# Token attention in the order plain, differential, neighbourhood mixer; one square root for both differential groups

## The reference

```
oa, oa_t = mixer_a(...)    # plain: 8 query heads, softmax over 768 keys
ob, ob_t = mixer_b(...)    # neighbourhood: 4 heads, a window of the 512 tokens by a bias, and the context
oc, oc_t = mixer_c(...)    # differential: 4 heads, w = p[0] - lam * p[1], then rms_norm(o, g_sub)
x = x + gt1_x * (concatenate([oa, ob, oc]) @ w_out[l])
```

## Time and profile before

| | |
|---|---|
| median of three executions | 3666.6 us (3666.44 to 3673.21) |
| profiled execution: its time | 3661.56 us |
| its span (first to last instruction) | 3659.7 us |
| TensorE busy | 3528.0 us, 96% of the span |
| VectorE, ScalarE, GpSimd busy | 48%, 42%, 40% |
| token attention, layer 0 | from 240.8 us to 474.7 us |
| token attention, layer 1 | from 1334.2 us to 1563.2 us |

### The profile page before, as it was taken

The page is one execution under the profiler, slowest core; times in us unless marked ns, Lnnn a source line. Parts: engine busy times, 40 slices in busy tenths (PEclk is TensorE's granted clock), DMA queues, the critical chain, the costliest instruction groups (busy, mean ns, idle before and its releaser), DMA issues.

```text
span 3659.7 us, 50085 instructions
## 1 busy us (share of the span) xinstructions
PE 3528.0 (96%) x19796; PEld 2799.3 (76%) x19796; DVE 1755.0 (48%) x2922; ACT 1524.8 (42%) x2557; POOL 1458.4 (40%) x986
## 2 busy tenths in 40 slices
PE   7999889999999999899999989999999989999998
PEld 5776567888899766578887768878887768888886
DVE  5766645423334766633542776161114686162114
ACT  4445554433455446534332355443223355443222
POOL 4520014444588510034444435344444444434442
PEclk8999999999999999999999999999999999999999
DMA  7613513333365411423333213223333213323331
GB/s 230 161 48 115 174 35 93 93 98 96 105 185 173 114 45 42 155 87 101 93 98 96 76 34 104 81 73 95 97 94 81 75 41 87 98 61 101 93 98 58
DMA packets 642466, 355.59 MB, mean 97 GB/s; under 512 B 70469, under 2 KB 614841, under 8 KB 642233
## 3 DMA queue, kind: packets, MB, share of 16 engines
q1 hardware_dynamic: 630379, 339.66, 32.2%
q10 hardware_dynamic: 11854, 12.72, 1.1%
HBM read 346.28 MB, written 6.05 MB: 96 GB/s over the span
## 4 chain that ended last, share of the span: by engine, by line
PE 89%; DVE 5%; ACT 3%; issue 2%; DMA 1%; POOL 1%; SPq 0%; ACTq 0%; DVEq 0%
PE psum L876 67%; PE psum L1105 5%; PE psum L1136 3%; PE psum L1156 2%; PE psum L900 1%; DVE neg_max L2013 1%; PE psum L1077 1%; ACT work L1574 1%; PE psum L980 1%; PE psum L904 1%; PE psum L1185 1%; PE psum L1036 1%; PE psum L931 1%; PE psum L1163 1%; PE psum L1015 1%
## 5 line engine op out<-in xcount | busy, mean ns | idle before, releaser
L859 POOL TENSOR_TENSOR w_lo<-w_raw,w_hi 128x256 fp32r<-128x256 f32 (+3 forms) x936 | 1396.5, 1512 | 2126.3 <-ACT w_hi L1413 2126.0
L876 PE MATMUL psum<-h_hi,w_hi 128*128 128x512 f32 (+1 forms) x2736 | 1034.2, 378 | 2.5 <-POOL w_lo L859 1.5
L876 PE MATMUL psum<-h_lo,w_hi 128*128 128x512 f32 (+1 forms) x2736 | 1010.1, 369 | 0.0
L876 PE MATMUL psum<-h_hi,w_lo 128*128 128x512 f32 (+1 forms) x2736 | 1010.1, 369 | 0.0
L1413 ACT ACTIVATE w_hi<-w_raw 128x1024 fp32r<-128x1024 f32 (+1 forms) x546 | 570.9, 1047 | 622.5 <-PE psum L876 587.6
L876 PEld LDWEIGHTS psum<-h_hi,w_hi 128*128 128x128 f32 x2736 | 516.5, 189 | 112.0 <-issue 19.8
L876 PEld LDWEIGHTS psum<-h_lo,w_hi 128*128 128x128 f32 x2736 | 516.5, 189 | 94.7 <-issue 9.9
L876 PEld LDWEIGHTS psum<-h_hi,w_lo 128*128 128x128 f32 x2736 | 516.2, 189 | 87.4
L876 PE MATMUL psum<-hid_hi,w_hi 128*128 128x512 f32 (+1 forms) x1040 | 393.0, 378 | 1.8 <-POOL w_lo L859 1.7
L876 PE MATMUL psum<-hid_lo,w_hi 128*128 128x512 f32 (+1 forms) x1040 | 391.8, 377 | 0.0
L876 PE MATMUL psum<-hid_hi,w_lo 128*128 128x512 f32 (+1 forms) x1040 | 391.8, 377 | 0.0
(11 more groups left out here) (248 smaller groups left out, 4280.1 us busy)
## 6 DMA issues: line engine op xcount, KB each, us to landing
w_raw<-in_w_up_dram SPq DMA_DIRECT2D x132, 512.0 KB, 3.8
w_raw<-in_w_ff_dram SPq DMA_DIRECT2D x128, 512.0 KB, 3.8
w_raw<-in_w_in_dram SPq DMA_DIRECT2D x92, 512.0 KB, 3.9
w_raw<-in_w_ada_dram SPq DMA_DIRECT2D x80, 512.0 KB, 4.2
w_raw<-in_w_down_dram SPq DMA_DIRECT2D x48, 512.0 KB, 3.6
w_raw<-in_w_mkv_dram SPq DMA_DIRECT2D x32, 512.0 KB, 3.9
w_raw<-in_w_down_dram SPq DMA_DIRECT2D x24, 384.0 KB, 3.1
w_ada_first<-in_w_ada_dram SPq DMA_DIRECT2D x4, 2048.0 KB, 18.0
```

What stands on the lines that cost most here:

```text
L859: m = nc.gpsimd.tensor_tensor(WL[:, c % NSPLIT, k:k + step, :], RAW[:, c % NRAW, k:k + step, :], WH[:, c % NSPLIT, k:k + step, :].bitcast( ...
L876: m = pe.matmul(out_ap, lhs(a, k), rhs(b, k), start=(k == 0 and n == 0), stop=(k == nk - 1 and n == 2))
```

## The change

The token plan is now 0 to 15 plain, 16 to 31 differential (groups 4 and 5), 32 to 39 neighbourhood (groups 6 and 7). The context plan keeps its order. The modulation ends with i = 31 and so starts four steps earlier: i = 8 to 31 in layer 0, 16 to 31 in layer 1. One square root over both groups' statistics (16 columns) stands at i = 35, and one reciprocal; the spreads stand at i = 36 and 37.

```
-ADA_LAST = 36
+ADA_LAST = 32
...
+            if stream == "x":
+                differential()
+                window()
+            else:
+                window()
+                differential()
...
+        def std_at(att):
+
+            return max(i for i, o in att["ends"].items() if att["groups"][o]["diff"] is not None) + 4 if att["wide"] else None
+
         def spread_at(att, i):
 
-            diff = [o for o, g in enumerate(att["groups"]) if g["diff"] is not None]
-            return [o for n, o in enumerate(diff) if i == len(att["steps"]) + 2 * n]
+            if att["wide"]:
+                return [o for n, o in enumerate(diff_groups(att)) if i == std_at(att) + 1 + n]
+            return [o for n, o in enumerate(diff_groups(att)) if i == len(att["steps"]) + 2 * n]
...
-                        pe.wait_ge(*at("sub_rstd", (S, o)))
+                        pe.wait_ge(*at("sub_rstd", S if att["wide"] else (S, o)))
...
+                    if att["wide"] and i == std_at(att):
+                        act.wait_ge(*at("sub_taken", (S, groups[diff_groups(att)[-1]]["bank"])))
+                        nc.scalar.activation(SUBS[:, :, :], SUBS[:, :, :], ACT.Sqrt, bias=EPSC[:, 0:1],
+                                             scale=1.0 / HEAD).then_inc(*mark("sub_std", S))
...
-                        if o and g["diff"] is None:
-                            dve.wait_ge(*at("o_lo", (S, o - 1)))
+                        if g["diff"] is None and plain_before(att, o) is not None:
+                            dve.wait_ge(*at("o_lo", (S, plain_before(att, o))))
...
+                    if att["wide"] and i == std_at(att):
+                        dve.wait_ge(*at("sub_std", S))
+                        nc.vector.reciprocal(SUBS[:, :, :], SUBS[:, :, :]).then_inc(*mark("sub_rstd", S))
```

More of the change, by code:

```diff
@@ L613, in attention_plan_1 @@
                 groups.append(dict(tile=m, diff=None))
[L614 to L632, removed]
+            def window():
+                for j in range(2):
+                    for t in range(nt):
+                        adds = [[], []]
+                        if stream == "x":
+                            adds = [[(0, SEQ, TB[:, 2 * j + lane, 6 - 2 * t:14 - 2 * t, :].rearrange("p a b -> p (a b)"))]
+                                    for lane in range(2)]
+                        steps.append(dict(lanes=[rows(64 * lane, 64, 5 + j, 7 + j, t) for lane in range(2)], nk=nk, adds=adds,
+                                          mix=None))
+                        turns.append(dict(parts=[(len(steps) - 1, 0), (len(steps) - 1, 1)], v=values(P + 128 * j), t=t,
+                                          group=len(groups)))
+                    groups.append(dict(tile=4 + j, diff=None))
@@ new lines, in differential @@
+            def differential():
+                for j in range(2):
+                    for t in range(nt):
+                        for e in range(2):
+                            steps.append(dict(lanes=[rows(64 * e + 32 * m, 32, 9 + j, 11 + j, t) for m in range(2)], nk=nk,
+                                              adds=[[], []], mix=layer))
+                        turns.append(dict(parts=[(len(steps) - 2, 1), (len(steps) - 1, 1)], v=values(384 + 128 * j), t=t,
+                                          group=len(groups)))
+                    groups.append(dict(tile=6 + j, diff=layer))
@@ L755, in finish_plan, with diff_groups, plain_before @@
             return att
+        def diff_groups(att):
+            return [o for o, g in enumerate(att["groups"]) if g["diff"] is not None]
+        def std_at(att):
+            return max(i for i, o in att["ends"].items() if att["groups"][o]["diff"] is not None) + 4 if att["wide"] else None
         def spread_at(att, i):
-            diff = [o for o, g in enumerate(att["groups"]) if g["diff"] is not None]
-            return [o for n, o in enumerate(diff) if i == len(att["steps"]) + 2 * n]
+            if att["wide"]:
+                return [o for n, o in enumerate(diff_groups(att)) if i == std_at(att) + 1 + n]
+            return [o for n, o in enumerate(diff_groups(att)) if i == len(att["steps"]) + 2 * n]
+        def plain_before(att, o):
+            before = [n for n in range(o) if att["groups"][n]["diff"] is None]
+            return before[-1] if before else None
         def sub_stats(att, o):
@@ L2071, in attend @@
                         lo("o_lo", (S, o), att_out(att, o, HL), diff_out(att, o), att_out(att, o, HH))
+                    if att["wide"] and i == std_at(att):
+                        dve.wait_ge(*at("sub_std", S))
+                        nc.vector.reciprocal(SUBS[:, :, :], SUBS[:, :, :]).then_inc(*mark("sub_rstd", S))
                     for o in spread_at(att, i):
-                        dve.wait_ge(*at("sub_std", (S, o)))
-                        nc.vector.reciprocal(sub_stats(att, o), sub_stats(att, o)).then_inc(*mark("sub_rstd", (S, o)))
+                        if not att["wide"]:
+                            dve.wait_ge(*at("sub_std", (S, o)))
+                            nc.vector.reciprocal(sub_stats(att, o), sub_stats(att, o)).then_inc(*mark("sub_rstd", (S, o)))
                         dve.wait_ge(*at("sub_spread", (S, o)))
```

2 lines of the change are left out of this document (1 added, 1 removed).

## The result

The changed kernel takes 3676.3 us (median of 20 runs, 3670.6 to 3689.7), the one before 3666.6 (20 runs beside it). The ratio is 1.0022, with a 95% interval of 1.0015 to 1.0029: **8.1 us slower, 5.5 to 10.6**. The forecast was 3667, a change too small to be told from none, with a range of 3658 to 3677. One of e10's 12 executions took 6983.69 us and is left out of its ratio.

What follows compares the result with a forecast made beforehand. TensorE was taken as the bound, carrying 89% of the chain. Layer 0's steps +9.0, layer 1's +3.0, ends -11.8, next stage -1.8 and slower clock +2 summed to +0.4 us: median 3667, range 3658 to 3677.

Steps and rivals of the forecast that it cites:

- The ends: From the last exponentials to TensorE's next stage: 5.6 us in each layer, -11.8 us in all.
- The start of the next stage: Projection of layer 1, behind a fuller end: -1.8 us there, nothing in layer 0.
- The plain steps: Steps 8 to 16: 53.6 us in layer 0 with more modulation, +4.3; 43.4 in layer 1, down from 44.72.
- The differential steps: Differential steps in their new place: +0.4 us in layer 0 for modulation in the last four, -0.6 in layer 1.
- Steps 32 to 39: Neighbourhood steps, now last: 55.3 us in each layer, added up step by step from queue waits.
- ScalarE's queue in step 36: Two table loads, square root, two copies and split delay step 36's exponentials: step 36 takes 6.9 us, +0.9.
- the table rival: Each of two table switches in both layers costs a second price of 1.28 us: +5, 3672 us; chance 8%.
- matmuls at half speed in these steps: Sign that the forecast is wrong: matmuls of the last steps running at TensorE's lower clock level.
- the wait in i = 34: TensorE's middle transpose waits for VectorE's copy of the sums of squares; extra price 1 us a layer, +2.
- The wait in i = 34 decides: Rival: that 2 us gap drops TensorE to 1.2 GHz, some 4.5 us a layer: +7 to +9, median 3674.5; chance 17%.
- Inner costs hidden: Rival: neighbourhood steps' idle time hides queued work and waits overlap: -8 us, 3658 and a tick; chance 17%.
- The modulation doesn't fit: Rival: modulation in the last four differential steps costs 3.9 us a layer, not 0.4: +7, 3673.5; chance 8%.

Runs made afterwards that it cites:

- e10: Changed kernel plus two filler matmuls over constants in each of TensorE's gaps at i = 32 and i = 34: 1.0007 against the kernel before, +2.6 us.
- e9: e8 with the modulation ending with step 33 instead of 31: 0.9980 against the kernel before, -7.3 us.
- e1: Kernel before with one edit, the modulation ending with step 31 instead of 35: 1.0019 against the kernel before, +7.0 us.
- e5: Changed kernel unchanged, run and profiled a second time: 1.0021 against the kernel before, +7.7 us.
- e11: Kernel before unchanged, profiled a second time: 3670.47 us.
- e6: Changed kernel with ScalarE's split of the first two w_out chunks in steps 33 and 34 instead of 36 and 37: 1.0021 against before, +7.7 us.
- e8: Changed kernel with the edits of e3, e6 and e7 together: 0.9996 against the kernel before, -1.5 us.
- e3: Changed kernel with VectorE's copy of the sums of squares between the step's two lanes instead of behind both: 0.9998 against before, -0.7 us.
- e7: Changed kernel with the spreads at i = 37 and 38 instead of 36 and 37: 1.0013 against the kernel before, +4.8 us.
- e4: Changed kernel with the square root at i = 40 and the spreads at 41 and 42, behind all steps: 1.0018 against before, +6.6 us.

## Why the prediction was right or wrong

**The ends: right.** 5.47 and 5.55 us where 5.6 was said. The chain of after goes through the steps that were named, in layer 1:

```profile
1569.09 0.66 PE psum L1159 x4
1569.75 1.46 PE psum L1179 x24
1571.21 0.59 PE psum L1159 x4
1571.79 1.02 PE psum L1208 x16
1572.82 1.31 PE psum L1179 x24
1574.13 43.74 PE psum L899 x192
```

**The start of the next stage: right.** The projection takes 43.74 us instead of 45.55, which is the -1.8 to the hundredth; windows over both ends have a clock of 1.00, where it was 0.85.

**The plain steps: right.** 53.7 us (mean of two) for steps 8 to 16 where 53.6 was said; 43.35 in layer 1 where 43.4 was.

**The differential steps: half right.** 83.7 forecast in layer 0, 85.7 measured; 82.7 and 82.1 in layer 1. The 2 us too much in layer 0 are in steps 26 and 27, behind the wait for the squares of the first differential group; the window of 387.40 above shows the clock of 0.54.

**Steps 32 to 39: right at full clock, wrong as they ran.** With the gaps filled (e10) they take 55.12 us in each layer; 55.3 was forecast. Step by step, forecast and e10 (layer 0): step 33 7.5 and 7.61; 35 7.7 and 7.28; 36 6.9 and 6.72; 37 7.4 and 7.56; 38 7.8 and 7.63; 39 6.1 and 5.96. ScalarE's queue in step 36, which the forecast wrote down row by row, stands in the timeline of after so:

```profile
448.96 1.28 ACT L1603 ACT_TABLE_LOAD   x1
450.26 0.31 ACT L1603 ACTIVATE sub_stats<-sub_stats,eps_cols 128x16 f32<-128x16 f32 x1
450.47 0.58 ACT L1567 ACTIVATE probs_t<-psum 128x512 f32<-128x512 f32 x1
450.95 1.05 ACT L1436 ACTIVATE w_hi<-w_raw 128x1024 fp32r<-128x1024 f32 x1
451.89 0.58 ACT L1567 ACTIVATE probs_t<-psum 128x512 f32<-128x512 f32 x1
452.50 1.28 ACT L1597 ACT_TABLE_LOAD   x1
453.79 0.90 ACT L1597 ACTIVATE work<-psum,neg_max 128x768 f32<-128x768 f32 x1
```

Next to each load the following instruction starts 0.02 us or less behind its end. The extra drain at each switch, by which the sum would have been +6, is not there, and the table rival falls: step 36 is 6.72 us in all profiles of after. That the total came out near that +6 is chance.

The range held, by 0.7 us: 3676.3 against 3677. But the forecast had named matmuls at half speed in these steps as a sign that it was wrong, and they came. **The step that failed** is the term in "Sum" on the wait in i = 34: "I take 1 us a layer, between 0 and 3: +2". What steps 32 to 39 took above their 55.12 at full clock is 1.35 us in layer 0 and 3.3 in layer 1 (means of two profiles), 4.6 us, and the half-speed stretch in the differential steps adds 2.0 that no term held. The forecast looked for gaps only where it had found a new wait. The gap in i = 32, of 2.11 us and longer than the one in i = 34, comes from work that is missing: no value product, and the modulation ended one step earlier. With modulation in it, it is 0.42 us (e9). The order of instructions would have shown it.

The other part of the miss does not lie in the steps. Against +0.4 the means of two profiles each give +8.75. Of these 8.35 us, the steps give 3.0 (their excess over the forecast, less the +2 that was in the sum, and less the 0.7 by which before's second profile was longer there), the middle 1.8, the rest of the kernel 2.3, the stretch up to step 7 in both layers 1.3. Up to step 7 and behind the ends TensorE's instructions are the same, and its largest waits in the rest are the same to 0.5 us each. What differs is the time at the lower clock level: a window's length, times two, times what its granted clock lacks to 1. Summed over short windows behind layer 1's projection:

| profile | us at 1.2 GHz | us to the end |
|---|---|---|
| before | 34.5 | 2050.9 |
| e1 (old order) | 41.4 | 2053.2 |
| after, second (e5) | 41.4 | 2053.6 |
| before, second (e11) | 44.8 | 2054.7 |
| e6 | 44.9 | 2054.6 |
| after | 51.6 | 2057.1 |
| e8 | 55.1 | 2058.7 |

The other six profiles lie on the same line, within 0.6 us: the length grows by 0.37 us for each us at the lower level. At equal time there, old and new order take the same. The middle, counted from the context attention's second scores, follows it too, more loosely (within 1.7 us): 10.6 us at the lower level and 860.0 in before, 17.3 and 863.3 in e11, 17.1 and 863.6 in after. Up to step 7, before has 27.3 us of it in both profiles, and after 34.1 and 30.7. So the 5.4 us of the miss that lie outside the steps go, in the main, with more time at the lower level in code that the change doesn't touch. **Why after's profiles have more of it stays open.** In the rest the three profiles with the old order have 34.5 to 44.8 us, the ten others 41.4 to 55.1. These ranges overlap, and two profiles of one kernel differ by 10, so chance and a carried effect of the new order can't be told apart. The whole span doesn't point at the new order: 113 and 144 us at the lower level before, 127 and 113 after.

**The rivals.** "The wait in i = 34 decides" had the right sign, size (+7 to +9) and sign of it (matmuls at half speed in these steps), and 17%. Its mechanism was half of it: it put all of it at one wait, and there are three gaps. Its size was chance: it came from 3.5 us a layer more in steps 33 to 39 than the forecast had, and there are 0.3 in layer 0 and 2.3 in layer 1 (the 1.35 and 3.3, less the 1 that the forecast took). "Inner costs hidden" was wrong: e3, e7 and e4 free each place for itself, and each gives what its queue says. "The modulation doesn't fit" is wrong in the differential steps of layer 1, which took less than forecast. The evidence used against the first rival, that neighbourhood steps in layer 1 leave 1.4 us idle each and keep 5.96, was true and did not bear on it: those steps have no gap of 2 us.

In e10 matmuls without use in two gaps, and nothing else, kept the granted clock of steps 32 to 39 at 1.00; the gaps behind which it fell were 1.4 to 2.1 us long. The Trainium skill (TensorE: Matmul & The Clock Gate, Part 1: The HAM clock gate) says that the clock follows how busy TensorE has recently been. The runs agree.

## What to carry to other kernels

When TensorE sets the end, list its gaps after a reordering, those from missing work as well as those from new waits, and price what stands behind each gap at both clock levels: here filling two gaps gave back 4.6 us in the steps (e10). Background work that costs nothing in a step with idle time may also hold up the clock there; moved into full steps it paid its own time, and the steps it left got no shorter in layer 0 and ran at a granted clock of 0.73 (e1, +7.0 us for one number). A copy that two engines need can stand better between the lanes of a step than behind them: moving one copy of 0.15 us gave 4.9 us in the steps and 8.4, give or take 5, in the total (e3), and with the spreads, the split and the modulation moved as well the new order beats the old one by 7.3 us (e9). Last, before calling a difference in untouched code unexplained, compare the time at the lower clock level in it.

## What was unexpected of the hardware

- Gaps of 1.97 and 2.11 us in TensorE were followed by matmuls at 1.2 GHz; the same gap in the next profile of the same kernel was followed by full speed in one layer (e5).
- Matmuls without use, 1.88 us of them in a gap of about 2.1 us (1.88 and the 0.25 left), shortened the steps around them by 4.6 us in two layers (e10).
- A stretch of about 2055 us with the same code takes 2050.9 to 2058.7 us, and nearly all of that spread goes with the time at the lower clock level in it, 34.5 to 55.1 us, at 0.37 us for each.
- Half speed is not always paid: behind layer 0's end before spent 3.4 us at the lower level between the context attention's first and second scores, after none, and these stood 4.00 and 3.95 us apart.
